# The x tiles of the first load move to the space of h_lo, and the rotary tables to a shared area loaded later

## The reference

```python
for l in range(2):
    mkv = mem_prompt @ w_mem_kv[l]              # 256 memory tokens, keys and values
    h = rmsnorm(x, g_pre)
    parts = split_cols(h @ w_in)                # one projection, 15 column groups
    a = c_b * conv3(c_c * c_x) * silu(c_z)                          # A: short conv
    b = rmsnorm(gated_linear_attention(g_q, g_k, g_v, g_lr)) * silu(g_z)      # B
    q, k = rope(s_q, pos), rope(s_k, pos)
    c = sliding_window_attention(q, k, s_v, window=128, sinks) * silu(s_z)    # C
    d = memory_attention(m_q, mk, mv) * silu(m_z)                   # D
    x = x + rmsnorm(concat(a, b, c, d) @ w_out, g_post)
```

## Time and profile before

| | us |
|---|---|
| median of 3 runs | 2507.32 |
| lowest and highest run | 2501.73, 2508.84 |
| the profiled execution, its own time | 2508.84 |
| its span, first to last instruction | 2507.0 |
| PE busy | 2396.2 |
| DVE busy | 1370.8 |
| ACT busy | 920.6 |

### The profile page before, as it was taken

One profiled execution on the slowest core, in us unless ns is written; L12 is line 12 of the kernel. 1 busy time (PEld: TensorE's weight loads), 2 busy tenths in 40 slices (PEclk: granted clock), 3 DMA queues, 4 the chain that ended last, 5 costly groups with the idle time before them and its releaser, 6 DMA issues. The chain is left out here.

```text
span 2507.0 us, 40561 instructions
## 1 busy us (share of the span) xinstructions
PE 2396.2 (96%) x14764; PEld 1913.0 (76%) x14764; DVE 1370.8 (55%) x3328; ACT 920.6 (37%) x2131; POOL 103.1 (4%) x175
## 2 busy tenths in 40 slices
PE   8999999999999999899999999999999999998998
PEld 4677777687787878778867777767877887787786
DVE  4466655555466654554635666465545665454443
ACT  4444223443444322333424442243434443232321
POOL 1000000000000000000000000000000000000000
PEclk9999999999999999999999999999999999898999
DMA  6111112243210212224331111223340113030322
GB/s 230 43 35 27 48 46 60 70 136 119 60 49 5 64 45 71 54 53 127 126 86 37 32 47 39 64 72 93 122 119 26 35 35 70 23 94 24 84 93 84
DMA packets 230784, 172.25 MB, mean 69 GB/s; under 512 B 56982, under 2 KB 207132, under 8 KB 230556
## 3 DMA queue, kind: packets, MB, share of 16 engines
q1 hardware_dynamic: 219668, 151.32, 21.2%
q10 hardware_dynamic: 10920, 18.33, 2.2%
HBM read 136.68 MB, written 21.93 MB: 63 GB/s over the span
## 5 line engine op out<-in xcount | busy, mean ns | idle before, releaser
L1537 PE MATMUL bank<-h_hi,w_hi 128*128 128x512 f32 (+3 forms) x2160 | 502.2, 371 | 24.1 <-ACTq L1893 8.5
L1537 PE MATMUL bank<-h_lo,w_hi 128*128 128x512 f32 (+3 forms) x2160 | 482.6, 363 | 1.7
L1537 PE MATMUL bank<-h_hi,w_lo 128*128 128x512 f32 (+2 forms) x2080 | 476.3, 367 | 1.3
L1537 PEld LDWEIGHTS bank<-h_hi,w_hi 128*128 128x128 f32 (+1 forms) x2160 | 362.0, 191 | 107.1 <-issue 51.1
L1537 PEld LDWEIGHTS bank<-h_lo,w_hi 128*128 128x128 f32 (+1 forms) x2160 | 357.9, 187 | 73.3 <-issue 13.0
L1537 PEld LDWEIGHTS bank<-h_hi,w_lo 128*128 128x128 f32 x2080 | 349.4, 192 | 62.7 <-issue 11.4
L2562 PE MATMUL bank<-scr_r,tb_r 128*128 128x512 f32 x816 | 195.1, 395 | 1.0 <-issue 1.0
L2562 PEld LDWEIGHTS bank<-scr_r,tb_r 128*128 128x128 f32 x816 | 151.7, 188 | 35.7 <-issue 2.3
L2562 PE MATMUL bank<-w_hi,tb_r 128*128 128x512 f32 x544 | 139.4, 401 | 0.0
L2258 DVE COPY_PREDICATED scr<-level_mask,bank 128x128 f32<-128x128 uint8 (+1 forms) x332 | 116.6, 351 | 33.7 <-PE bank L1648 16.0
L2100 DVE TENSOR_TENSOR w_lo<-w_raw,w_hi 128x1024 fp32r<-128x1024 f32 x92 | 112.4, 1222 | 38.8 <-ACT w_hi L1870 33.3
(11 more groups left out here) (290 smaller groups left out, 3261.8 us busy)
## 6 DMA issues: line engine op xcount, KB each, us to landing
w_raw<-in_w_in SPq DMA_DIRECT2D x96, 512.0 KB, 3.7
out<-scr SPq DMA_DIRECT2D x32, 512.0 KB, 2.6
scr<-in_w_out SPq DMA_DIRECT2D x16, 512.0 KB, 5.5
w_raw<-in_w_out SPq DMA_DIRECT2D x16, 512.0 KB, 3.8
scr<-in_x_prompt SPq DMA_DIRECT2D x16, 512.0 KB, 3.6
scr<-out SPq DMA_DIRECT2D x16, 512.0 KB, 3.2
rot<-out ACTq DMA_DIRECT2D x12, 512.0 KB, 3.3
mix_t<-in_x_prompt ACTq DMA_DIRECT2D x8, 512.0 KB, 13.8
```

Source lines behind the costliest of these rows:

```text
L1537: m = mm(bank[b][0:m_w, 0:c1 - c0], w[:, slot, k, 0:m_w], h[:, k, c0:c1], start=it["piece"] == 0 and k == 0, stop=it["piece"] == 2 and k = ...
```

## The change

In `start` the x tiles no longer lie in `mix_t` but in `x_first`, a second name with another type for the space of `h_lo`. Tile t is `x_first[:, :, P*t:P*t+P]`: 8 blocks of 128 floats in each partition, 1088 floats apart, exactly the place to which `h_lo` of the same tokens is written afterwards. `level_f32` moves from `tb` to `mix_t`.

The rotary tables become one area `tab` in `scr`, cos and sin of 1088 tokens each, which overlaps the gate's `la` and `b`. They are loaded after the last `fac_dist` item of B(1), second step, and SP waits for its distances and exponentials. In the second passes the tables of the sample tokens are loaded there too, with two DMAs more, and `tab_s` and its two loads in `start` are gone. The staging of the outgoing keys and values, `out_kv`, moves from `low` to `scr`.

```diff
-TAB = layout([("cos", PASS)], GLA_P["end"][0])
-TAB.update(layout([("sin", PASS)], GATE_P["end"][0]))
-STAGE = layout([("in", 2 * GW)], TAB["sin"][0])
+TAB = layout([("tab", 2 * TOK)], GLA_P["end"][0])
+STAGE = layout([("kv", 8 * HD)], TAB["end"][0])
@@ head() of the planner
         for i, n in enumerate(groups_n):
             out.append(item("fac_dist", step=s, i=i, n=n))
+        if (s["unit"], s["g"], s["st"]) == ("B", 1, 1):
+            out.append(item("tables", step=s))
         for i, n in enumerate(groups_n):
             out.append(item("fac_prod", step=s, i=i, n=n, last=i == len(groups_n) - 1))
@@ planner, at "begin"
-            if it["slot"] == TABLES_AT:
-                emit(item("tables", slot=it["slot"]))
@@ tiles
-    h_lo = sb(ctx, "h_lo", [P, KT, TOK], F32R)
+    x_first, h_lo = twice(ctx, "x_first", F32, "h_lo", F32R, [P, KT, TOK])
-    tab_s = sb(ctx, "tab_s", [P, 2, NS])
@@ start()
-        level_f32 = tb[:, 1].rearrange("p r n -> p (r n)")[:, 0:(NL + 1) * CH].rearrange("p (n t) -> p n t", n=NL + 1)
+        level_f32 = mix_t[:, 0, 0:(NL + 1) * CH].rearrange("p (n t) -> p n t", n=NL + 1)
-                  (seq_one[:], k_seq), (tab_s[:, 0], k_cos[:, SEQ:SEQ + NS]), (tab_s[:, 1], k_sin[:, SEQ:SEQ + NS])]
+                  (seq_one[:], k_seq)]
         def x_of(t):
-            return mix_t[:, t, 0:D]
+            return x_first[:, :, P * t:P * t + P]
@@ start(), PE
-                        m = nc.tensor.transpose(bank[b][:, (k % 4) * P:(k % 4 + 1) * P], x_of(t)[:, k * P:(k + 1) * P], ident[:])
+                        m = nc.tensor.transpose(bank[b][:, (k % 4) * P:(k % 4 + 1) * P], x_of(t)[:, k], ident[:])
@@ units(), SP
                 elif it["kind"] == "tables":
-                    all_steps_done(sp, it["slot"])
-                    for name, src in (("cos", k_cos), ("sin", k_sin)):
-                        o, n = TAB[name]
-                        sp.dma_start(scr[:, o:o + n], src[:, tok0:tok0 + PASS]).then_inc(table_in, 16)
+                    s = it["step"]
+                    sp.wait_ge(dist_done, dist_before[s["n"]] + len(groups_of(s)) + 1)
+                    sp.wait_ge(decay_done, decays_before(s) + len(groups_of(s)) + 2)
+                    for i, src in enumerate((k_cos, k_sin)):
+                        sp.dma_start(tab[:, i, 0:PASS], src[:, tok0:tok0 + PASS]).then_inc(table_in, 16)
+                        if second:
+                            sp.dma_start(tab[:, i, PASS:TOK], src[:, SEQ:SEQ + NS]).then_inc(table_in, 16)
@@ units(), DVE, rope_k (rope_q likewise)
-                    dve.wait_ge(table_in, 16 * 2)
+                    dve.wait_ge(table_in, 16 * (4 if second else 2))
-                    tt(key_copy(s), key_copy(s), table(s, 0), ALU.mult)
+                    tt(key_copy(s), key_copy(s), tab[:, 0, c0:c1], ALU.mult)
```

More of the change, by code:

```diff
@@ L117 @@
                 ("sq", NS), ("r", NS)], SWA_S["kct"][0])
-TAB = layout([("cos", PASS)], GLA_P["end"][0])
-TAB.update(layout([("sin", PASS)], GATE_P["end"][0]))
-STAGE = layout([("in", 2 * GW)], TAB["sin"][0])
+TAB = layout([("tab", 2 * TOK)], GLA_P["end"][0])
+STAGE = layout([("kv", 8 * HD)], TAB["end"][0])
 OUT_S = layout([("res", D), ("normed", D), ("wo_hi", RING * KT * P), ("wo_lo", RING * KT * P)])
 SCRATCH = OUT_S["end"][0]
-assert TAB["end"][0] <= SCRATCH
-assert max(MEM_S["kc"][0] + NB * 2 * P, TAB["cos"][0] + PASS) <= GATE_P["la"][0]
-assert max(SWA_S["end"][0], GLA_S["end"][0]) <= TAB["cos"][0]
+assert STAGE["end"][0] <= SCRATCH
+assert max(MEM_S["kc"][0] + NB * 2 * P, GLA_P["end"][0]) <= GATE_P["la"][0]
+assert max(SWA_S["end"][0], GLA_S["end"][0]) <= TAB["tab"][0] and GATE_P["end"][0] <= STAGE["kv"][0]
 PE_SEES, PE_SEEN = 0.25, 0.12
@@ L342, in piece_needs @@
         return p + PE_SEES
-TABLES_AT = 2
 ROWS = {"A": (0, 1, 2, 3), "B": (0, 1, 2, 3), "C": (0, 1, 2, 3), "D": (0, 3)}
@@ L931, in start @@
         w_kv = scr[:, KT * NMEM:KT * NMEM + DEPTH * KT * 2 * GW].rearrange("p (i k n) -> p i k n", i=DEPTH, k=KT)
-        squared = tb[:, 0].rearrange("p r n -> p (r n)")[:, 0:D]
+        squared = tb[:, 0].rearrange("p r n -> p (r n)")[:, 0:D].rearrange("p (k t) -> p k t", k=KT)
         order = [("mem",), ("h", 0), ("kv", 0, 0), ("h", 1), ("kv", 1, 0), ("h", 2), ("kv", 0, 1), ("h", 3), ("kv", 1, 1), ("h", 4),
@@ L1057, in on_vector @@
             ts, tt, stt = nc.vector.tensor_scalar, nc.vector.tensor_tensor, nc.vector.scalar_tensor_tensor
+            g = pre_g.rearrange("p (k t) -> p k t", k=KT)
             dve.wait_ge(pre_in, 16)
@@ L1066, in norm @@
                 dve.wait_ge(root_done, t + 1)
-                stt(x_of(t), x_of(t), z[:, 3:4], pre_g, ALU.mult, ALU.mult).then_inc(xn_done, 1)
+                stt(x_of(t), x_of(t), z[:, 3:4], g, ALU.mult, ALU.mult).then_inc(xn_done, 1)
             def w_low(i):
@@ L1115, in units @@
         out_c = low[64:80, 0:4 * P].rearrange("p (i g n) -> p i g n", i=2, g=2)
-        o, _ = STAGE["in"]
+        o, n = STAGE["kv"]
         conv_st = scr[0:2 * NB, o:o + GW]
         mem_k = scr[:, o:o + 2 * GW].rearrange("p (c n) -> p c n", c=2)
[L1119 to L1126, removed]
+        out_kv = scr[:, o:o + n].rearrange("p (j i g d) -> p j i g d", j=2, i=2, g=2)
+        o, n = TAB["tab"]
+        tab = scr[:, o:o + n].rearrange("p (i t) -> p i t", i=2)
         def area(lay, name, parts=slice(0, P)):
@@ L2326, in on_vector @@
                     s = it["step"]
-                    dve.wait_ge(table_in, 16 * 2)
+                    c0, c1 = cols(s)
+                    dve.wait_ge(table_in, 16 * (4 if second else 2))
                     dve.wait_ge(key_in[s["st"]], key_need[s["n"]])
-                    tt(key_copy(s), key_copy(s), table(s, 0), ALU.mult)
-                    link(tt(key_turned(s), key_turned(s), table(s, 1), ALU.mult))
+                    tt(key_copy(s), key_copy(s), tab[:, 0, c0:c1], ALU.mult)
+                    link(tt(key_turned(s), key_turned(s), tab[:, 1, c0:c1], ALU.mult))
                     tt(key_copy(s), key_copy(s), key_turned(s), ALU.add).then_inc(key_done, 1)
@@ L2334, in on_vector @@
                     s = it["step"]
+                    c0, c1 = cols(s)
                     q, qt = buf(s, "q"), query_turned(s)
                     dve.wait_ge(query_in[s["st"]], query_need[s["n"]])
-                    tt(qt, qt, table(s, 1), ALU.mult)
-                    link(tt(q, q, table(s, 0), ALU.mult))
+                    tt(qt, qt, tab[:, 1, c0:c1], ALU.mult)
+                    link(tt(q, q, tab[:, 0, c0:c1], ALU.mult))
                     tt(q, q, qt, ALU.add).then_inc(rot_done, 1)
```

## The result

The changed kernel takes 2575.69 us, the median of 4 runs (2573.80 to 2577.07), against 2506.89 us of the kernel before, here the median of 4: 1.0277 times, 95% interval 1.0260 to 1.0295. It is slower by 68.8 us. The prediction was 2531.4 us and its range ended at 2539: the sign was right, the size was not, by 44.3 us.

The account below looks back on a forecast made before the run. TensorE was taken as the bound, busy 2396.2 of 2507.0 us. The profiled 2508.8 plus 20.5 (start) and 3.6 (tables) gave 2532.9, less 1.5 for the median 2531.4 us; range 2514 to 2539.

Parts of the forecast that it names:

- The cut and the sharing: Start: x loads cut into 512 B packets, 1024 a tile instead of 128; the two queues alternate packet for packet.
- the 110 against 111: Start, kernel before, 21 to 22 us: 110 packets of 4 KB beside 111 of 64 B, cited for one-for-one sharing.
- the sharing by bytes: Rival for the start: ACT held, but queues share by bytes; restart 14.8 us later, 2526 us, chance 0.06.
- I take 30.4: Start: the moment in us when ACT's last x issue ends, held by its full queue.
- the term of the start: Start: PE restarts at 37.6 us instead of 17.10 because ACT is held issuing x loads, +20.5 us.
- the other number: Start: with 2316 open packets as the limit instead of 2786, ACT's issue ends at 33.6 us.
- the 2316 of the earlier trace: Start, kernel before: packets open on SP's queue at 17.52 us; at 23.75 us 2786 were open.
- the 36.2 us of fixed chain: Start: PE's unbroken work from 17.10 us to the first projection at 53.29, expected to keep its length.
- PE loses 1.8 us: C(0)'s head, passes one and three: table 3.0 us late for rope_k, 1.2 us covered; 3.6 us for both passes.
- 30 us of cover, nothing: Passes two and four: last distance at 826.91 us, first key copy at 858.21, so the moved tables cost nothing.
- Up to 3.3 us more, kept for the range: Possible half-clock stretch behind a PE wait, as the 6.60 us one at 282.96; not in the sum.
- The sum: Whole kernel: 2508.8 + 20.5 for the start + 3.6 for the tables = 2532.9 us; as a median 2531.4.

Follow-up runs that it names:

- x_late: x_only, but ACT issues x tiles 2 to 7 one by one between its squares instead of all ahead of them: 2511.76 us, ratio 1.0020.
- x_cut: Kernel before, x tiles still in mix_t and issued as before, only viewed in eight pieces of 128 columns: 2534.60 us, ratio 1.0106.
- x_only: Kernel before with only the x tiles moved to x_first and level_f32 to mix_t: 2527.58 us, ratio 1.0094.
- tab_second_late: tab_only, but in passes two and four the tables are issued at the begin of slot 5, behind two w_in tiles: 2531.81 us, ratio 1.0104.
- tab_only: Changed kernel with the x part taken back, so only the tables part and out_kv's move remain: 2553.83 us, ratio 1.0192.

## Why the prediction was wrong

**The cut and the sharing: right.** The x loads came in 8608 packets, as counted. By 33.3 us ACT's queue had done 6222 packets and SP's 6417, though ACT's were mostly of 512 B and SP's of 64 B to 4 KB. The Trainium skill ("DMA: Bandwidth & Descriptors", Queues, rings and completion order) gives one queue 9 to 17 descriptors before the next has its turn. With 4101 packets of one queue beside 4114 of the other between 13 and 27 us of the changed kernel, these counts can't show how long a turn is, and neither can the 110 against 111 that the prediction set against the rule. What both exclude is the sharing by bytes that was made of it as a rival.

**"I take 30.4": the term of the start was too small, 20.5 against 25.3 us.** The issue ended at 33.35, as by the other number, 33.6: 8608 - 6222 leaves 2386 packets open, close to the 2316 of the earlier trace rows and not to the 2786. That is 3.0 us. From there to PE's restart it was 8.0 us and not 7.2, and the 36.2 us of fixed chain became 37.2, since PE was at half clock until 47.3. `x_late` and `x_cut` confirm the mechanism. The total was met in part by luck: the medians give 20.8 us for `x_only`, close to 20.5, but 28.6 for `x_cut`, which has the same start. Behind the start the lag doesn't stay as it is. In the trace of `x_only` it is 24.5 us at the projections, 21.6 at 780 us and 31.6 at the end, as short stretches at half clock come and go. One of 10.2 us at 824.0, which the kernel before doesn't have, costs 4.1.

**"PE loses 1.8 us" in passes one and three: roughly right as a wait.** rope_k waited 4.29 us for the table in pass one, forecast at 3.0, and PE 2.43 and 2.73.

**"30 us of cover, nothing" in passes two and four: wrong.** The argument asked when the tables are wanted, and not what stands behind them. SP's queue is in a written order; four loads, together 1.1 MB, ahead of a tile of `w_in` for which ACT already waited 0.60 us before, make PE wait 2.64 and 2.18 us. `tab_second_late` changes nothing but the tables' place in this order and gets 22.0 us back. The prediction counted the issues that the tables were moved behind, and left out those that they were moved ahead of.

**"Up to 3.3 us more, kept for the range": the step that failed, by its size.** The sum had the stretch at nothing, and the range at 3.3 us. That bound came from the one stretch in the earlier trace rows, 6.60 us behind a wait of 1.01 us, and was put on waits forecast at 1.8. The runs show stretches of 13.6 to 30.7 us behind waits of 2.1 to 3.2 at this place. Ten operations on DVE cost 13.9 us a wait, 2.7 of them the wait. By this price four waits are some 56 us, and the tables part measured 47.0; the prediction had 3.6.

The sum by its own terms, then: 20.8 to 28.6 for the x part (forecast 20.5), 47.0 for the tables (forecast 3.6). Of the missing 44.3 us nearly all is in the second. The kind of effect had been named, but one row was used as its ceiling, and it wasn't even the longest in the trace of the kernel before. The timeline of PE at 2262 us and the stretch behind it:

```profile
2262.34 0.33 PE L1625 MATMUL bank<-spare 64*64 64x64 f32 x4 [1.66 <-DVE scr L2233]
```

```profile
2263.60:2277.20 13.60, 12.50 (x36) 8.26 (x36) 4.89 (x10) 2.17 (x5) 0.00 (x0) 0.50 0.00 1
```

With a second wait of 1.10 us inside it, this stretch is twice as long as the one in the earlier trace rows. PE was busy for 12.50 us of it, so it lost up to 6.3 us. As a ceiling that is still only about half of the 11.2 us that each stretch behind the ten operations cost.

**What stays open.** Why the stretch is 27 us behind one wait of this length and 13.6 behind another. The length of the wait doesn't decide it alone. In the kernel before PE waits 3.74 us among projections and then has half clock for only 6.8:

```profile
465.93 2.05 PE L1537 MATMUL bank<-h_hi,w_hi 128*128 128x512 f32 x4 [3.74 <-ACTq L1893]
```

```profile
464.80:471.60 6.80, 5.67 (x15) 4.55 (x16) 5.31 (x12) 2.85 (x6) 0.00 (x0) 0.50 0.00 0
```

Behind that wait come mostly matmuls of 512 columns, behind those in slot 5 mostly groups of 64 x 64 and 128 x 128 with a few of 512 between. That the kind of work has a part in how long the half clock lasts is argued from these rows; no run put the same wait ahead of another kind of work. It can't be all: in pass four the changed kernel and `tab_only` have the same 2.18 us ahead of the same matmuls, and 13.6 against 27.3 us at half clock.

## What to carry to other kernels

When a transfer is moved in a queue, ask two questions: what is it late for, and what is late behind it; the second cost more here than the first was thought to. Price a new wait on TensorE by the longest stretch at half clock that the trace has behind a wait of such a length, and not by the first one found. If the trace has none, make one with a few operations on unused data and measure it before relying on a bound. A view that cuts a DMA's target into short runs costs most on the engine that issues it: put the issues between that engine's computations, or leave them to a queue that has nothing else to do.

## What the hardware showed that was not expected

- PE stayed at half clock while it was busy 27.30 of 27.30 us. The Trainium skill ("TensorE: Matmul & The Clock Gate", Part 1) has the clock go by how busy PE has lately been; the rows agree that a wait brings it down, but not that being busy brings it back, as PE was never idle in that stretch. Nor is a wait always needed: in the kernel before the clock fell to 0.50 at 693.4 us, though PE had been busy for all of the 9.4 us before; since 690.91 it was at 64 matmuls of 8 columns.
- At one place the step is steep. PE waits of 0.83, 1.25 and 1.78 us at the begin of slot 5 in pass one had no half clock in the 16 us behind them in the profiled executions; 2.14, 2.43, 2.70 and 2.77 us had 27.3 us at 0.50, and 2.53 us had 30.7. It isn't a threshold for other places: in the kernel before 1.66 us had 13.6. Kernels between the two, with 1.25 and 1.78, have runs that spread over 32 and 22 us. With 0.83 they spread over 13 us, about as those of the kernel before, and the four runs with 2.70 over 2.
- An issuing engine was held for 30.30 us by seven loads of 512 KB in packets of 512 B, with some 2390 packets open when it came free. With the same loads in packets of 4 KB it was free after 3.90 us.
